# A gated recurrence in chunks: outputs of two heads as one block-diagonal product, and the next chunk's scores ahead of them

## The chip, the cores and the metric

The kernel runs on one core of a Trainium2 chip. The metric is the device time of one execution in microseconds (us); before the change it is the median of three runs. All matrix products are in fp32 on TensorE (PE in the profile). PSUM is the memory that PE writes, in eight banks; VectorE is DVE, ScalarE is ACT, GpSimd is POOL. In this program each engine has an instruction list of its own, carried out in order, and the lists meet at named semaphores.

## The reference

The program is a two-layer attention block followed by a block with three mixers and an MLP. The change lies in one mixer of the second block, the gated linear recurrence: 4 heads, 64 keys and 64 values each, 9 chunks of 128 tokens (the first holds padding and 16 meta tokens; its outputs are not used).

```python
def step(S, inp):
    q_c, k_c, v_c, g_c = inp
    gcum = jnp.cumsum(g_c, axis=1)
    seg = gcum[:, :, None] - gcum[:, None, :]
    decay = masked_decay(seg, causal[None, :, :, None, None])
    scores = jnp.einsum('bthk,btshk,bshk->btsh', q_c, decay, k_c)
    o_intra = jnp.einsum('btsh,bshv->bthv', scores, v_c)
    o_inter = jnp.einsum('bthk,bhkv->bthv', q_c * jnp.exp(gcum), S)
    k_end = k_c * jnp.exp(gcum[:, -1:] - gcum)
    S = S * jnp.exp(gcum[:, -1])[..., None] + jnp.einsum('bshk,bshv->bhkv', k_end, v_c)
    return S, o_intra + o_inter
```

## The kernel before

Everything here is in `stage_hg` (from L2653 on), where the list of each engine is written out by hand. The four heads are two pairs (`fb` 0 and 1); in a pair, head `e` has partitions 64*e to 64*e+63. The score of two tokens needs a decay that depends on both, so it is taken in levels: the chunk is halved again and again, and on each level queries and keys are scaled to the middle of their half. For chunk i the work is:

- `sums(i, fb)` (PE, L2670): three products of 384 columns into banks 0 to 2 give the sums of log decays on all levels. ACT takes their exponential (L2757, `EX`). DVE multiplies it with the queries (`q_levels`, L2799, `Qt`), POOL with the keys (L2785, `Kl`).
- `end_sums(i)` (PE, L2680): decays to the chunk's end, into columns 384 to 511 of banks 0 and 1; ACT's exponential (L2766, `EE`), then POOL's product with the keys (L2778, `kend`).
- `scores(i, fb)` (PE, L2693): 16 products, 8 for each head, with 64 rows each, into banks 4 to 7. There is one set of these banks, so the scores of a pair wait until DVE has taken the scores of the pair before.
- `merge(i, fb)` (DVE, L2816): 14 copies under a mask, 7 for each head, put the right level for every pair of tokens into `Sm`.
- `outputs(i, h)` (PE, L2711 and L2715), one head at a time: two products of `Sm` with the values (128 columns of moving data), and one of the scaled query with the head's state (64 rows, 64 columns), accumulated in bank 3. DVE copies the result out (L2836).
- the state sum (PE, L2745): `kend` times values, four products, into columns of banks 0 and 1; DVE scales the state and adds it (L2841, 64 columns for each pair).

A matrix product in the program is two MATMUL and two LDWEIGHTS instructions in the trace. `Sm` has one buffer, used by both pairs in turn, so `merge(i, 1)` waits for the first two outputs, which read pair 0's.

Of the kernel before, what the change touches and what calls it, by code (L numbers as in the profile page):

```python
# [15 lines left out]
ALU = mybir.AluOpType  # L16
# [4 lines left out]
P = 128  # L21
# [12 lines left out]
HD = 64  # L34
# [2618 lines left out]
def stage_hg(pr, qk, Kt, LF, Vh, OH, c, b_):  # L2653
# [8 lines left out]
    with nc.Block() as block:  # L2662
        @block.tensor
        def _(pe):
# [9 lines left out]
            def end_sums(i):  # L2674

                if i >= 1:
                    pe.wait_ge(*S["state_new"](i))
                    pe.wait_ge(*S["decayed"](2 * i + 2))
                for fb in range(2):
                    mm = pe.matmul(ps[:, fb, TW:BANK], c["gt"], LF[:, i, fb * P:(fb + 1) * P], start=True, stop=True)  # L2680
                mm.then_inc(*S["end_sums"].inc())
# [24 lines left out]
            def outputs(i, h):  # L2706
                fb, r = h // 2, slice(64 * (h % 2), 64 * (h % 2) + 64)
                j = (i - 1) * HGH + h
                pe.wait_ge(*S["masked"](4 * ((i - 1) * 2 + fb) + 3 + h % 2))
                for half in range(2):  # L2710
                    pe.matmul(ps[:, 3, h * P:h * P + WIDE], Sm[:, h % 2, half, :], Vh[:, i, h * HD:h * HD + WIDE],  # L2711
                              start=(half == 0), stop=False, skip_group_check=True)
                if j >= 1:
                    pe.wait_ge(*S["o_ready"](j))
                pe.matmul(ps[:, 3, h * P:h * P + HD], Qt[r, i % 2, fb, LEVELS, :], st[r, fb, :], start=False, stop=True,  # L2715
                          skip_group_check=True).then_inc(*S["o_ready"].inc())
# [3 lines left out]
            for i in range(n):  # L2720
                if i >= 1:
                    scores(i, 0)
                else:
                    pe.wait_ge(*S["decayed"](2))
                end_sums(i)
# [3 lines left out]
                if i >= 2:  # L2729
                    pe.wait_ge(*S["o_used"](i - 1))  # L2730
                if i >= 1:
                    outputs(i, 0)
                    scores(i, 1)
                if i + 1 < n:
                    sums(i + 1, 1)
                if i >= 1:
                    for h in range(1, HGH):
                        outputs(i, h)
                pe.wait_ge(*S["kend_ready"](i + 1))
                if i + 1 < n:  # L2740
                    pe.wait_ge(*S["decayed"](2 * i + 4))
                for fb in range(2):
                    for half in range(2):
                        at = fb * P + 64 * half
                        mm = pe.matmul(ps[64 * half:64 * half + 64, fb, TW:TW + HD], kend[:, at:at + 64], Vh[:, i, at:at + HD],  # L2745
                                       start=True, stop=True)
                mm.then_inc(*S["state_sum"].inc())
# [41 lines left out]
        def _(dve):  # L2789
            masks = c["pairs"].bitcast(mybir.dt.int32).rearrange("p (v n) -> p v n", v=LEVELS)  # L2790

            def q_levels(i, fb):
# [3 lines left out]
                if i >= 1:  # L2796
                    if i >= 3:
                        dve.wait_ge(*S["o_ready"](HGH * (i - 2)))
# [4 lines left out]
            def merge(i, fb):  # L2803
# [3 lines left out]
                for v in range(LEVELS):  # L2807
                    for e in range(2):
                        tile = (e, v % 2)
                        if v == 0:  # L2810
                            dve.wait_ge(*S["scored"](j + e + 1))
                            if j + e >= 2:
                                dve.wait_ge(*S["o_ready"](j + e - 1))
                        if tile in last:
                            dve.wait_ge(*S["dve"](last[tile]))
                        ins = dve.copy_predicated(Sm[:, e, v % 2, :], masks[:, v, :], ps[:, 4 + 2 * e + v // 4, v % 4 * P:(v % 4 + 1) * P])  # L2816
# [8 lines left out]
            dve.wait_ge(*S["state_zero"](2))  # L2825
            q_levels(0, 0)
            q_levels(0, 1)
            for i in range(n):
# [5 lines left out]
                if i >= 1:  # L2834
                    dve.wait_ge(*S["o_ready"](HGH * i))
                    dve.tensor_copy(OH[:, i - 1, :].rearrange("p (h d) -> p h d", h=HGH),  # L2836
# [362 lines left out]
```

## Time and profile before

| | us |
|---|---|
| median of three runs (lowest, highest) | 4134.05 (4129.21, 4137.35) |
| the profiled execution | 4127.2 |
| its span | 4125.4 |
| `stage_hg`, from its first matmul to its last state update | 171.48 |
| TensorE busy over the span | 3849.8 |
| TensorE busy in `stage_hg` | 139.29 |

The span runs from the first to the last recorded instruction of the profiled execution. A busy time sums instructions that may overlap between engines. The granted TensorE clock is a share of 2.4 GHz; its two levels are 1.0 and 0.5. DMA is idle in `stage_hg`: nothing is loaded there.

### The profile page before, as it was taken

The numbers are of one execution on the slowest core, as the hardware profiler recorded it, in microseconds if no ns is written. First come the engines' busy times: TensorE is split into PE (matmuls) and PEld (weight loads), VectorE is DVE, ScalarE is ACT, GpSimd is POOL, SyncE is SP. The second block draws the span as 40 slices with busy tenths as digits, with TensorE's granted clock in tenths as the row PEclk, the third lists the DMA queues.
The fourth block names the chain that finished last, engine by engine and source line by source line (L and its number), as shares of the span: only waits on it lengthen the run. The fifth ranks groups of instructions, "written<-read, shape, count | busy, mean of one in ns | idle before, by whom it ended". The sixth has DMA issues, their size and how long they took to land. (4 is left out here: it accounts for less than half of the span.)

```text
span 4125.4 us, 50459 instructions
## 1 busy us (share of the span) xinstructions
PE 3849.8 (93%) x19200; PEld 2376.3 (58%) x19200; DVE 2006.8 (49%) x4125; ACT 1284.2 (31%) x2388; POOL 698.3 (17%) x868
## 2 busy tenths in 40 slices
PE   5999999999998999899999899999787999999998
PEld 3655556756644655577565456656365488438843
DVE  3377456633534476465243303545244444674465
ACT  3245325523522344354243113442711211001100
POOL 2400230021004000501100001123032000430043
PEclk8999999999999999999999999999987999999999
DMA  4101240001021110100112200000100222452244
GB/s 176 44 19 37 103 149 16 2 16 68 25 71 41 52 37 27 66 1 1 36 48 72 72 31 21 21 21 1 41 1 22 89 90 97 163 183 98 86 163 153
DMA packets 108942, 253.71 MB, mean 61 GB/s; under 512 B 5200, under 2 KB 33872, under 8 KB 108320
## 3 DMA queue, kind: packets, MB, share of 16 engines
q1 hardware_dynamic: 103056, 231.86, 16.0%
q10 hardware_dynamic: 4384, 12.58, 0.8%
q0 software_dynamic: 1264, 6.04, 0.4%
q8 instruction: 156, 2.56, 0.3%
q14 instruction: 82, 0.67, 0.1%
HBM read 223.20 MB, written 27.26 MB: 61 GB/s over the span
## 5 line engine op out<-in xcount | busy, mean ns | idle before, releaser
L674 PE MATMUL ps<-ring,hT 128*128 128x384 f32 (+3 forms) x2208 | 692.4, 471 | 17.2 <-PEq L268 6.1
L674 PEld LDWEIGHTS ps<-ring,hT 128*128 128x128 f32 x2208 | 395.3, 195 | 274.0 <-issue 145.6
L1086 DVE TENSOR_REDUCE stat_a<-ps 128x1 f32<-128x1280 f32 (+1 forms) x144 | 196.6, 1368 | 178.9 <-PE ps L945 178.7
L984 PE MATMUL ps<-hT,ring 128*128 128x512 f32 (+1 forms) x640 | 280.2, 551 | 0.0
L1598 PE MATMUL ps<-ring,YT 128*128 128x512 f32 x576 | 250.2, 592 | 1.3 <-PEq L1363 1.3
L1026 ACT ACTIVATE YT<-ps,stat_a 128x1280 f32<-128x1280 f32 (+1 forms) x144 | 177.6, 1233 | 199.7 <-DVE stat_a L1086 197.7
L1962 ACT ACTIVATE hid<-hid 128x1024 f32<-128x1024 f32 x32 | 33.8, 1058 | 549.6 <-DVE hid L2042 549.6
L1982 POOL TENSOR_TENSOR Wd<-ring 128x512 f32<-128x512 f32 x64 | 85.5, 1335 | 678.1 <-DMA ring<-in_w_down 604.4
L1940 PE MATMUL ps<-Wd,const 128*128 128x512 f32 x384 | 185.9, 593 | 0.1
L1598 PEld LDWEIGHTS ps<-ring,YT 128*128 128x128 f32 x576 | 108.1, 190 | 131.4 <-issue 131.4
L1919 PE MATMUL ps<-Hc,Wu 128*128 128x256 f32 x768 | 171.0, 379 | 0.0
L441 PE MATMUL ps<-ring,hT 128*128 128x512 f32 (+1 forms) x432 | 160.1, 530 | 5.4 <-DMA ring<-in_w_in 5.1
L1919 PEld LDWEIGHTS ps<-Hc,Wu 128*128 128x128 f32 x768 | 145.9, 190 | 19.8
L1940 PE MATMUL ps<-ring,hid 128*128 128x512 f32 x256 | 133.3, 602 | 11.0 <-PE ps L1940 4.4
L1185 PE MATMUL ps<-qk_b 64*128 64x512 f32 (+1 forms) x600 | 124.0, 545 | 20.1 <-ACT P_b L1260 17.9
L1215 PE MATMUL ps<-const,P_b 128*128 128x128 f32 x984 | 136.6, 278 | 2.2 <-DVE YT L1125 1.8
L955 PEld LDWEIGHTS ps<-const,YT 128*128 128x128 f32 x656 | 69.1, 142 | 120.7 <-issue 105.1
L1250 ACT ACTIVATE PT_b<-ps 128x512 f32<-128x512 f32 x150 | 84.5, 596 | 166.0 <-PE ps L1215 166.0
L1919 PE MATMUL ps<-hT,ring 128*128 128x256 f32 x512 | 120.8, 390 | 15.7 <-DVE hT L2061 6.6
L1260 ACT ACTIVATE P_b<-ps,stat_b 128x1280 f32<-128x1280 f32 (+1 forms) x108 | 132.8, 1235 | 6.4 <-DVE stat_b L1300 6.4
L984 PEld LDWEIGHTS ps<-hT,ring 128*128 128x128 f32 x640 | 106.3, 191 | 40.1 <-issue 37.7
L2153 PE MATMUL ps<-hT,ring 128*128 128x348 f32 (+1 forms) x384 | 129.4, 466 | 0.0
(451 smaller groups left out, 6860.8 us busy)
## 6 DMA issues: line engine op xcount, KB each, us to landing
ring<-in_w_down SPq DMA_DIRECT2D x32, 2048.0 KB, 7.9
ring<-in_w_up SPq DMA_DIRECT2D x16, 2048.0 KB, 8.1
ring<-in_w_in SPq DMA_DIRECT2D x14, 2048.0 KB, 7.9
adaw_b<-in_w_ada SPq DMA_DIRECT2D x16, 1024.0 KB, 5.2
ring<-in_w_out SPq DMA_DIRECT2D x6, 2048.0 KB, 7.9
ring<-in_w_in SPq DMA_DIRECT2D x6, 1536.0 KB, 6.8
x<-res SPq DMA_DIRECT2D x18, 512.0 KB, 2.9
gates<-const SPq DMA_DIRECT2D x32, 256.0 KB, 2.4
```

What stands on the lines that cost most here:

```text
L441: mm = pe.matmul(ps[:, n % 2, 0:width], hT[:, k, t * P:(t + 1) * P], w[:, k, :], start=(k == 0), stop=(k == KC - 1))
L674: mm = pe.matmul(ps[:, n % 2, 0:hi - lo], hT[:, k, t * P:(t + 1) * P], w[:, k, lo:hi], start=(k == 0), stop=(k == KC - 1))
L984: mm = pe.matmul(ps[:, GB, 0:hi - lo], pr.view(i0 + c)[:, k, b % 4 * P:(b % 4 + 1) * P], hT[:, k, lo:hi], start=(k == 0), stop=(k == KC - 1))
L1026: act.activation(dst, scored_at(i, m), ACT.Exp, bias=st[:, i % 4, m:m + 1], accum_out=st[:, i % 4, 2 + m:3 + m])\
L1086: dve.tensor_reduce(st[:, i % 4, m:m + 1], scored_at(i, m), AX, ALU.max, negate=True)\
L1185: return pe.matmul(flat[:, at:at + width], qk[r, u["qb"], u["qt"] * P:(u["qt"] + 1) * P], qk[r, u["kb"], key:key + width], start=True, sto ...
L1215: mm = pe.transpose(ps[:, bank, (i - lo) * P:(i - lo + 1) * P], Pb[:, p % 2, e, b * P:(b + 1) * P], ident)
L1260: act.activation(Pb[:, p % 2, e, 0:nk[p] * P], scored_at(p, e), ACT.Exp, bias=st[:, p % 4, e:e + 1], accum_out=st[:, p % 4, 2 + e:3 + e]). ...
L1598: mm = pe.matmul(ps[:, 2 * (m % 2) + h, :], YT[:, k, t * P:(t + 1) * P], w[:, k, :], start=(k == 0), stop=(k == KC - 1))
L1919: mm = pe.matmul(up_at(n, x), a[:, k, :], b[:, k, :], start=(k == 0), stop=(k == 3))
L1940: mm = pe.matmul(ps[:, down_bank(pair, x), :], a, b, start=(j == 0), stop=(j == PAIRS - 1))
L2153: mm = pe.matmul(ps[:, dense_bank(u), 0:hi - lo], w[:, k, (b % 4) * P:(b % 4 + 1) * P], hT[:, k, lo:hi], start=(k == 0), stop=(k == KC - 1))
```

## The change

Both pairs get their own half of `Sm` (`[P, 2, 2, 2, P]`). The state becomes a tile of 128 columns for each pair, with the two heads' blocks on its diagonal and zeros elsewhere. `outputs(i, fb)` does a pair at a time: one product with 128 rows and 128 columns takes both heads' scaled queries through the state, and four products of 64 columns add `Sm` times values. The state sums move from banks 0 and 1 into the free half of bank 3, whose off-diagonal blocks are cleared once; the state update now reads 128 columns for each pair. TensorE's list is written in another order: the first scores of chunk i + 1 and its end sums come ahead of the second outputs and the state sum of chunk i. DVE's copy of the outputs comes behind its wait for the state sum.

```diff
@@ -2673,9 +2673,7 @@
...
-                if i >= 1:
-                    pe.wait_ge(*S["state_new"](i))
-                    pe.wait_ge(*S["decayed"](2 * i + 2))
+                pe.wait_ge(*S["decayed"](2 * i + 2))
                 for fb in range(2):
@@ -2703,48 +2701,49 @@
...
-            def outputs(i, h):
-                fb, r = h // 2, slice(64 * (h % 2), 64 * (h % 2) + 64)
-                j = (i - 1) * HGH + h
-                pe.wait_ge(*S["masked"](4 * ((i - 1) * 2 + fb) + 3 + h % 2))
-                for half in range(2):
-                    pe.matmul(ps[:, 3, h * P:h * P + WIDE], Sm[:, h % 2, half, :], Vh[:, i, h * HD:h * HD + WIDE],
-                              start=(half == 0), stop=False, skip_group_check=True)
-                if j >= 1:
-                    pe.wait_ge(*S["o_ready"](j))
-                pe.matmul(ps[:, 3, h * P:h * P + HD], Qt[r, i % 2, fb, LEVELS, :], st[r, fb, :], start=False, stop=True,
-                          skip_group_check=True).then_inc(*S["o_ready"].inc())
+            def outputs(i, fb):
+                if fb == 0:
+                    pe.wait_ge(*S["state_new"](i))
+                pe.wait_ge(*S["masked"](4 * place(i - 1, fb)))
+                pe.matmul(ps[:, 3, fb * P:(fb + 1) * P], Qt[:, i % 2, fb, LEVELS, :], st[:, fb, :], start=True, stop=False,
+                          skip_group_check=True)
+                for h in range(2 * fb, 2 * fb + 2):
+                    for half in range(2):
+                        mm = pe.matmul(ps[:, 3, h * HD:(h + 1) * HD], Sm[:, fb, h % 2, half, :], Vh[:, i, h * HD:(h + 1) * HD],
+                                       start=False, stop=(half == 1), skip_group_check=True)
+                mm.then_inc(*S["o_ready"].inc())
+            def state_sum(i):
+                pe.wait_ge(*S["kend_ready"](i + 1))
+                for fb in range(2):
+                    for half in range(2):
+                        r, at = slice(64 * half, 64 * half + 64), fb * P + 64 * half
+                        mm = pe.matmul(ps[r, 3, 2 * P + at:2 * P + at + HD], kend[:, at:at + 64], Vh[:, i, at:at + HD],
+                                       start=True, stop=True, skip_group_check=True)
+                mm.then_inc(*S["state_sum"].inc())
...
             sums(0, 1)
-            for i in range(n):
-                if i >= 1:
-                    scores(i, 0)
-                else:
-                    pe.wait_ge(*S["decayed"](2))
-                end_sums(i)
+            end_sums(0)
+            pe.wait_ge(*S["end_decayed"](1))
+            sums(1, 0)
+            sums(1, 1)
+            scores(1, 0)
+            end_sums(1)
+            pe.wait_ge(*S["state_zero"](3))
+            state_sum(0)
+            for i in range(1, n):
                 if i + 1 < n:
...
                     sums(i + 1, 0)
-                if i >= 2:
-                    pe.wait_ge(*S["o_used"](i - 1))
-                if i >= 1:
-                    outputs(i, 0)
-                    scores(i, 1)
+                scores(i, 1)
+                outputs(i, 0)
                 if i + 1 < n:
                     sums(i + 1, 1)
-                if i >= 1:
-                    for h in range(1, HGH):
-                        outputs(i, h)
-                pe.wait_ge(*S["kend_ready"](i + 1))
-                if i + 1 < n:
-                    pe.wait_ge(*S["decayed"](2 * i + 4))
-                for fb in range(2):
-                    for half in range(2):
-                        at = fb * P + 64 * half
-                        mm = pe.matmul(ps[64 * half:64 * half + 64, fb, TW:TW + HD], kend[:, at:at + 64], Vh[:, i, at:at + HD],
-                                       start=True, stop=True)
-                mm.then_inc(*S["state_sum"].inc())
+                    scores(i + 1, 0)
+                    end_sums(i + 1)
+                outputs(i, 1)
+                state_sum(i)
@@ -2787,6 +2786,7 @@
...
         def _(dve):
+            sums_at = ps[:, 3, 2 * P:BANK]
             masks = c["pairs"].bitcast(mybir.dt.int32).rearrange("p (v n) -> p v n", v=LEVELS)
@@ -2795,7 +2795,7 @@
...
                     if i >= 3:
-                        dve.wait_ge(*S["o_ready"](HGH * (i - 2)))
+                        dve.wait_ge(*S["o_ready"](place(i - 3, fb)))
                     dve.tensor_tensor(Qt[:, i % 2, fb, :, :], EX[:, fb, 0:LEVELS + 1, :],
@@ -2809,11 +2809,11 @@
...
                             dve.wait_ge(*S["scored"](j + e + 1))
-                            if j + e >= 2:
-                                dve.wait_ge(*S["o_ready"](j + e - 1))
+                            if i >= 2:
+                                dve.wait_ge(*S["o_ready"](place(i - 2, fb)))
                         if tile in last:
                             dve.wait_ge(*S["dve"](last[tile]))
-                        ins = dve.copy_predicated(Sm[:, e, v % 2, :], masks[:, v, :], ps[:, 4 + 2 * e + v // 4, v % 4 * P:(v % 4 + 1) * P])
+                        ins = dve.copy_predicated(Sm[:, fb, e, v % 2, :], masks[:, v, :], ps[:, 4 + 2 * e + v // 4, v % 4 * P:(v % 4 + 1) * P])
                         if v < LEVELS - 2:
@@ -2822,7 +2822,8 @@
...
             dve.memset(st[:], 0.0).then_inc(*S["state_zero"].inc())
-            dve.wait_ge(*S["state_zero"](2))
+            dve.memset(sums_at, 0.0).then_inc(*S["state_zero"].inc())
+            dve.wait_ge(*S["state_zero"](3))
             q_levels(0, 0)
@@ -2831,15 +2832,14 @@
...
                         q_levels(i + 1, fb)
-                if i >= 1:
-                    dve.wait_ge(*S["o_ready"](HGH * i))
-                    dve.tensor_copy(OH[:, i - 1, :].rearrange("p (h d) -> p h d", h=HGH),
-                                    ps[:, 3, :].rearrange("p (h d) -> p h d", h=HGH)[:, :, 0:HD]).then_inc(*S["o_used"].inc())
                 dve.wait_ge(*S["q_levels"](place(i, 1)))
                 dve.wait_ge(*S["state_sum"](i + 1))
+                if i >= 1:
+                    dve.wait_ge(*S["o_ready"](place(i - 1, 1)))
+                    dve.tensor_copy(OH[:, i - 1, :], ps[:, 3, 0:2 * P])
                 for fb in range(2):
                     ins = dve.scalar_tensor_tensor(out=st[:, fb, :], in0=st[:, fb, :], scalar=dec[:, i % 2, fb:fb + 1],
-                                                   in1=ps[:, fb, TW:TW + HD], op0=ALU.mult, op1=ALU.add)
+                                                   in1=sums_at[:, fb * P:(fb + 1) * P], op0=ALU.mult, op1=ALU.add)
                 ins.then_inc(*S["state_new"].inc())
@@ -3132,7 +3132,7 @@
...
                         "decay": sv("decay", P, 2, 2), "EE": sv("EE", P, 256), "kend": sv("kend", P, 256),
-                        "Sm": sv("Sm", P, 2, 2, P), "state": sv("state", P, 2, HD)})
+                        "Sm": sv("Sm", P, 2, 2, 2, P), "state": sv("state", P, 2, P)})
             with ExitStack() as w:
...
```

TensorE in the middle of the stage, before: from the second sums of a chunk (L2670) over the outputs of three heads (L2711, L2715) and the state sum (L2745) to the first scores of the next (L2693).

```order
L2670 MATMUL ps<-const,LF_hg 128x384 x3
L2711 MATMUL ps<-V,Sm_hgc 128x128 x2
L2715 MATMUL ps<-state_hgc,hT 128x64
L2711 MATMUL ps<-V,Sm_hgc 128x128 x2
L2715 MATMUL ps<-state_hgc,hT 128x64
L2711 MATMUL ps<-V,Sm_hgc 128x128 x2
L2715 MATMUL ps<-state_hgc,hT 128x64
L2745 MATMUL ps<-V,kend_hgc 64x64 x4
L2693 MATMUL ps<-hT 128x128 x2
L2693 MATMUL ps<-hT 64x64 x2
L2693 MATMUL ps<-hT 128x128 x10
L2693 MATMUL ps<-qk_hg 128x128 x2
```

The same stretch after the change; L2691 are scores, L2678 end sums, L2708 and L2712 the two kinds of output product, L2721 the state sum.

```order
L2670 MATMUL ps<-const,LF_hg 128x384 x3
L2691 MATMUL ps<-hT 128x128 x2
L2691 MATMUL ps<-hT 64x64 x2
L2691 MATMUL ps<-hT 128x128 x10
L2691 MATMUL ps<-qk_hg 128x128 x2
L2678 MATMUL ps<-LF_hg,const 128x128 x2
L2708 MATMUL ps<-state_hgc,hT 128x128
L2712 MATMUL ps<-V,Sm_hgc 128x64 x4
L2721 MATMUL ps<-V,kend_hgc 64x64 x4
L2670 MATMUL ps<-const,LF_hg 128x384 x3
```

The first scores and the end sums of the next chunk stand between the second sums and the outputs of the second pair; these outputs are one product and four instead of three times two and one.

DVE in the same stretch with what it waits for, before: the masks of the second pair, the query levels, the copy of the outputs (L2836), the state update (L2841), the next masks.

```order
L2816 COPY_PREDICATED Sm_hgc<-const,ps 128x128 [waits o_ready,scored] x2
L2816 COPY_PREDICATED Sm_hgc<-const,ps 128x128 x2
L2816 COPY_PREDICATED Sm_hgc<-const,ps 128x128 [waits dve] x10
L2799 TENSOR_TENSOR hT<-EX_hgc,qk_hg 128x1024 [waits o_ready,decayed]
L2801 COPY decay_hgc<-EX_hgc 128x1
L2836 COPY O_hg<-ps 128x256 [waits o_ready]
L2841 SCALAR_TENSOR_TENSOR state_hgc<-state_hgc,decay_hgc,ps 128x64 [waits state_sum,q_levels]
L2841 SCALAR_TENSOR_TENSOR state_hgc<-state_hgc,decay_hgc,ps 128x64
L2816 COPY_PREDICATED Sm_hgc<-const,ps 128x128 [waits o_ready,scored,state_new]
```

After the change:

```order
L2816 COPY_PREDICATED Sm_hgc<-const,ps 128x128 [waits o_ready,scored] x2
L2816 COPY_PREDICATED Sm_hgc<-const,ps 128x128 x2
L2816 COPY_PREDICATED Sm_hgc<-const,ps 128x128 [waits dve] x10
L2799 TENSOR_TENSOR hT<-EX_hgc,qk_hg 128x1024 [waits o_ready,decayed]
L2801 COPY decay_hgc<-EX_hgc 128x1
L2839 COPY O_hg<-ps 128x256 [waits o_ready,state_sum,q_levels]
L2841 SCALAR_TENSOR_TENSOR state_hgc<-state_hgc,decay_hgc,ps 128x128 x2
L2816 COPY_PREDICATED Sm_hgc<-const,ps 128x128 [waits o_ready,scored,state_new]
```

The order is the same; the copy of the outputs now also waits for the state sum, and the update has 128 columns.

## Rows read from the trace of the kernel before

**Rows 1.** The page's busy times over the span.

```profile
PE 3849.8 (93%) x19200; PEld 2376.3 (58%) x19200; DVE 2006.8 (49%) x4125; ACT 1284.2 (31%) x2388; POOL 698.3 (17%) x868
```

**Rows 2.** Stretches of the stage: PE, PEld, DVE, ACT, POOL busy, clock, DMA, GB/s.

```profile
2979.65:3151.13 171.48, 139.29 (x920) 104.45 (x920) 75.14 (x286) 23.82 (x27) 48.86 (x25) 0.82 0.00 1
3021.04:3033.71 12.67, 10.04 (x69) 7.36 (x69) 6.92 (x26) 2.26 (x2) 5.87 (x3) 1.00 0.01 2
3110.60:3131.10 20.50, 17.39 (x115) 13.43 (x113) 9.22 (x35) 2.65 (x3) 5.88 (x3) 0.75 0.00 1
3131.10:3151.13 20.03, 15.05 (x102) 12.56 (x100) 7.21 (x33) 0.38 (x1) 0.73 (x1) 0.67 0.00 1
```

**Rows 3.** Waits in the stage: who for whom, total us, times, longest.

```profile
PE ps L2711 <- DVE Sm_hgc L2816: 22.8, 9, 2.6
DVE Sm_hgc L2816 <- PE ps L2715: 20.2, 8, 2.7
```

**Rows 4.** Timeline of one chunk at full clock: start, us, instruction, [idle before].

```profile
3021.04 2.21 PE L2670 MATMUL ps<-const,LF_hg 128*128 128x384 f32 x6 [0.47 <-ACT EE_hgc L2766]
3023.08 0.61 PE L2711 MATMUL ps<-V,Sm_hgc 128*128 128x128 f32 x4
3023.28 1.13 ACT L2757 ACTIVATE EX_hgc<-ps 128x1152 f32<-128x1152 f32 x1 [2.29 <-PE ps L2670]
3023.63 0.37 PE L2693 MATMUL ps<-hT 64*128 64x128 f32 x1
3024.44 1.22 DVE L2799 TENSOR_TENSOR hT<-EX_hgc,qk_hg 128x1024 f32<-128x1024 f32 x1 [1.93 <-ACT EX_hgc L2757]
3026.05 2.21 PE L2670 MATMUL ps<-const,LF_hg 128*128 128x384 f32 x6
3026.16 0.30 DVE L2816 COPY_PREDICATED Sm_hgc<-const,ps 128x128 f32<-128x128 int32 x1 [0.42 <-PE ps L2693]
3029.17 2.67 DVE L2816 COPY_PREDICATED Sm_hgc<-const,ps 128x128 f32<-128x128 int32 x13 [2.71 <-PE ps L2715]
3031.70 0.71 PE L2711 MATMUL ps<-V,Sm_hgc 128*128 128x128 f32 x4 [2.63 <-DVE Sm_hgc L2816]
3033.71 0.54 PE L2745 MATMUL ps<-V,kend_hgc 128*64 128x64 f32 x8
3033.82 0.42 DVE L2836 COPY O_hg<-ps 128x256 f32<-128x256 f32 x1 [0.79 <-PE ps L2715]
3034.17 3.48 PE L2693 MATMUL ps<-hT 64*128 64x128 f32 x28
3034.35 0.47 DVE L2841 SCALAR_TENSOR_TENSOR state_hgc<-state_hgc,decay_hgc,ps 128x64 f32<-128x64 f32 x2
3037.80 0.71 PE L2680 MATMUL ps<-LF_hg,const 128*128 128x128 f32 x4
3038.99 0.59 PE L2670 MATMUL ps<-const,LF_hg 128*128 128x384 f32 x1 [0.47 <-ACT EE_hgc L2766]
```

**Rows 5.** Timeline, the same operations in stretches of half clock.

```profile
2989.18 3.87 PE L2670 MATMUL ps<-const,LF_hg 128*128 128x384 f32 x6 [0.47 <-ACT EE_hgc L2766]
3015.49 3.64 PE L2693 MATMUL ps<-hT 64*128 64x128 f32 x28
3019.48 0.79 PE L2680 MATMUL ps<-LF_hg,const 128*128 128x128 f32 x2
3128.71 0.93 PEld L2711 LDWEIGHTS ps<-V,Sm_hgc 128*128 128x128 f32 x4
```

**Rows 6.** Timeline of earlier stages: products of narrow and of 128-column data.

```profile
517.49 0.61 PE L631 MATMUL ps<-const,row_b 128*128 128x2 f32 x4
517.95 1.10 PE L674 MATMUL ps<-ring,hT 128*128 128x512 f32 x2
...
2810.48 1.89 PE L2557 MATMUL ps<-xdt_ssd,W_ssd 128*128 128x128 f32 x16
```

**Rows 7.** Timeline, the first product of key levels on POOL.

```profile
2994.30 3.11 POOL L2785 TENSOR_TENSOR hT<-EX_hgc,qk_hg 128x896 f32<-128x896 f32 x1 [4.36 <-ACT EX_hgc L2757]
```

## The prediction

> **What bounds the kernel now.** I began with the page's busy times: TensorE is busy in 3849.8 of 4125.4 us [rows 1], so it sets the time of the program as a whole, and only what it does or waits for inside the changed stage counts. The stretches of the stage come next. It takes 171.48 us, 4.2% of the span. TensorE's records cover 139.29 us of it, DVE's 75.14, and the granted clock is 0.82, which with levels of 1.0 and 0.5 (2.4 and 1.2 GHz) means half clock in 36% of the time [rows 2]. DMA moves nothing there. Then the waits: DVE's masks wait 20.2 us for the outputs of the pair before, which still read `Sm`, and TensorE's outputs then wait 22.8 us for the masks [rows 3]. That is one stall of about 2.6 us a chunk.
>
> The timeline of a chunk shows what ends last. In the stretch from 3021.04 to 3033.71 the granted clock is 1.00 [rows 2]. TensorE runs without a break from the level sums to the output of the second head; DVE's masks start at 3029.17, and TensorE's outputs go on at 3031.70 after 2.63 us of nothing [rows 4]. One more wait of 0.47 us stands in each chunk between the end sums and the next level sums, for ACT's exponential [rows 4]. At 3034.17 comes the next chunk.
>
> The length of a chunk at full clock, from these rows: 3034.17 - 3021.04 = 13.13 us; the scores, 3026.05 - 3023.63 = 2.42; end sums and the wait for ACT, 3038.99 - 3037.80 = 1.19. Together 16.74 us [rows 4]. The measured length is (3131.10 - 3015.49) / 6 = 19.27 us [rows 2, 5]. So half clock costs 2.53 us a chunk.
>
> **The change, part by part.** Durations at full clock.
>
> *Outputs.* Before, two heads take 3033.71 - 3031.70 = 2.01 us, and the first head of a chunk 0.55 (3023.08 to 3023.63), since scores start beside its last product: 0.55 + 3 x 1.0 = 3.55 us a chunk [rows 4]. Now a pair is 5 products, 10 instructions. Four of the five move 64 columns instead of 128. Does this halve them? Products with 128 columns of weights and only 2 moving columns stand 0.46 / 4 = 0.115 us apart, and those with 128 moving columns take at most 1.89 / 16 = 0.118 [rows 6]. The loading of weights sets the pace, so the narrow ones gain nothing. I take 0.112 each, 1.12 a pair, and 0.17 for the change between 64 and 128 rows: a head has six instructions, 0.67, in its 1.0, and the other 0.33 lies in two such changes. So 1.29 a pair, 2.58 a chunk: 0.97 less on TensorE. Bounds for a pair: 0.7 (the eight narrow ones at half the pace, 2 x 0.112 + 8 x 0.056) and 2.01 (what two heads take now).
>
> By the Trainium skill, "TensorE: Matmul & The Clock Gate", section "Back-to-back issue gap", a matmul of up to 64 columns takes about 60 cycles, under half of one with 128; its section "LDWEIGHTS (loading the stationary operand)" has the load go by weight columns, 128 here whatever moves. By the first a pair would take 0.4 us less and the total some 5 us less; the trace agrees with the second, with 0.115 us for 2 moving columns [rows 6].
>
> *The order.* Call T the start of `scores(i, 0)`. Then, on TensorE: scores 2.42, end sums 4 x 0.112 = 0.45, outputs of pair 1 of the chunk before 1.29, and 0.64 from the start of the state sum to when DVE can read it (3033.71 to 3034.35) [rows 4]: T + 4.80. DVE, whose list has the copy and the state update ahead of the next masks, stands idle until then, though the scores were ready at T + 2.53 (3023.63 to 3026.16). Its copy takes 0.45, the update of twice 128 columns 0.60 (bounds 0.47, what two of 64 take now, and 0.84, two copies of 256 columns) and 0.10 to settle: masks start at T + 5.95. They take 2.87 (2.67 for 13 and 0.20 for one) [rows 4], to T + 8.82. TensorE meanwhile does the state sum and the next level sums, 2.04 (3021.04 to 3023.08) [rows 4], to T + 6.7, and must wait for the masks, since `scores(i, 1)` go into the same banks: idle for 2.15 us. Scores from T + 8.85, masks of pair 1 from 11.38 to 14.25. TensorE: 8.85 + 2.42 + 1.29 + 2.04 = 14.60. The later of the two, 14.60, is the next T. So both chains are nearly even, and the stall has not gone: it was 2.63 + 0.47 and is 2.15, and it now stands before `scores(i, 1)`.
>
> The gain of structure is 16.74 - 14.60 = 2.1 us a chunk: 0.97 of outputs, 0.95 of waits, the rest of changes of shape. What would be late next is covered: the level sums that end at T + 6.7 give an exponential (1.13) by T + 8.1 [rows 4], and POOL's product, 3.11 at most [rows 7], ends by T + 11.3, ahead of 14.60. DVE's own (1.22) lies between the two sets of masks, 8.82 to 11.38 [rows 4]. ACT's exponential of the end sums is done before T + 4, so that the level sums no longer wait for it.
>
> *End sums in bank 0 and 1, state sums in bank 3.* The end sums lose their wait for the state update, which was never last. No cost either way: DVE reads bank 3 (T + 4.8 to 5.9) while TensorE writes bank 0.
>
> *More to clear.* 512 more columns of `Sm` and 256 of bank 3. A DVE operation on 256 columns takes 0.42 [rows 4], so under 1.3 us, while TensorE does the first level sums, up to 3.87 at half clock [rows 5]. Nothing.
>
> *Start.* The first product of levels on POOL ends at 2994.30 + 3.11 = 2997.41 [rows 7]; `scores(1, 0)` start at 2997.45. The state sum comes behind scores and end sums, at 3000.4, DVE's update ends at 3001.7, masks 3004.5, scores, then 2.42 + 1.29 + 2.04 for TensorE: `scores(2, 0)` at 3010.3. Before: 3015.49 [rows 5]. 5.2 us earlier.
>
> *End.* From the eighth chunk's T: masks of pair 1 end at 14.25, outputs 1.29, state sum 0.64, copy and update 1.05: 17.2. Before it was 20.03 at a clock of 0.67 [rows 2]. With some half clock I take 18.8: 1.2 less.
>
> *The clock.* This is the unknown. Half clock costs 2.53 us a chunk now, with 3.1 us idle. In proportion to the idle time it would cost 2.53 x 2.15 / 3.1 = 1.8. Below, 0: the clock stays up. Above, 4. I take 1.8, the value nearest to the rows, since the stall is nearly as long as the one after which the clock falls today. A chunk is then 16.4 us, six chunks 98.4 against 115.6.
>
> *Sum.* 5.2 + 17.2 + 1.2 = 23.6 us less. The stage would take 148 us. The profiled execution took 4127.2 us and would take 4103.6. It lies 6.85 below the median of the three runs; 4134.05 - 23.6 gives 4110.
>
> **The rivals.**
>
> *A: the clock stays up.* Before the stall the scores take 2.42 in all, at 3034.17, behind it, 3.48 for all but the last four instructions [rows 4]: the clock falls after the stall. If 2.15 us are too short for a fall, a chunk takes 14.6: six are 87.6, 28.0 less; start 5.2, end 2.8. 36 us less, 4098. For it: shorter idle time in one piece. Against it: it is only 0.5 us shorter than the longest one now. In the Trainium skill, "TensorE: Matmul & The Clock Gate", section "Loop structure matters more than you think", the clock stays up when matmuls follow each other densely; by that rule moving scores into the gap would give this case. That the trace has a clock of 1.00 up to the stall and 3.48 us for scores behind it [rows 2, 4] agrees, but the new order keeps a stall.
>
> *B: more half clock than now.* Each chunk has work that DVE's chain waits for right behind the stall (`scores(i, 1)`), so a fall there lengthens both chains. At 3 to 4 us of loss a chunk takes 17.6 to 18.6: 4 to 10 less over six; with start and end 8 to 16 us less, 4122. For it: at half clock level sums take 3.87 and scores 3.64 and more [rows 5]. Against: the idle time of a chunk is 1 us less than now.
>
> *C: slower.* The stage falls to half clock for good. Then scores take 3019.48 - 3015.49 = 3.99, level sums 3.87, four output instructions 0.93, so ten and a shape change 2.6 [rows 5]. To T': 3.99 + 0.9 + 2.6 + 0.8 = 8.3, copy, update and masks 4.0, scores 3.99, outputs 2.6, level sums 3.87: 22.8 us a chunk, 3.5 more than the 19.27 now. Six: 21 more, and at the ends what order gains, half clock takes: 4155. It decides when half clock fills over 57% of a chunk ((19.27 - 14.6) / (22.8 - 14.6)). The last chunks now stand at 0.75 and 0.67 [rows 2], 50% and 66% of half clock, which keeps this alive; but these are after longer stalls.
>
> *D: only TensorE's work counts.* If DVE's update or its masks start later than I think, by more than 1.5 us, the whole gain of order is lost and the 0.97 x 8 = 8 us of outputs are left: 4126.
>
> **How the numbers follow.** The forecast has a chance of 0.60 (15 to 31 us less, 4103 to 4119), A 0.16, B 0.11, D 0.08, C 0.05. The range is 4096 to 4124: it holds the forecast, most of A and part of B, and about 0.15 is left out. This kernel's runs spread by 0.2% (8 us), which I take for what can be told from no change. Faster by over that: forecast, A and most of B, 0.86. Within it: D and a rest of B, 0.09. Slower: C, 0.05.
>
> **What would show it.** In the changed profile: ten output instructions in about 1.1 us, not 0.7; the outputs' wait for masks gone, and a wait of about 2.1 us of the scores of pair 1 in its place; DVE idle for over 3 us in each chunk until the state sum; chunks of 14.6 us where the clock is 1.00; a granted clock over the stage near 0.85. Wrong would be a chunk of over 16 us at full clock, a wait of the scores for POOL's levels, or a clock below 0.7.

## The result, and the profile after

| | before | after |
|---|---|---|
| median, us (lowest, highest; runs) | 4135.7 (4129.21, 4137.45; 4) | 4103.7 (4099.38, 4111.16; 4) |
| ratio to before (95% interval) | 1 | 0.9927 (0.9909, 0.9946) |
| profiled execution, us (span) | 4127.2 (4125.4) | 4111.16 (4109.3) |
| `stage_hg`, us | 171.48 | 144.38 |
| behind the stage to the span's end, us | 974.3 | 973.8 |

The forecast, 4110 in 4096 to 4124, came from the first three runs before; the table has a fourth. Run again beside the experiments the changed kernel gave 0.9936 (0.9920, 0.9952) and a stage of 144.35.

The two profiled spans differ by 16 us, the stages by 27: the stage begins at 2991.15 in this profile and at 2979.65 in that of before, so the part ahead of it, which the change does not touch, took 11.5 us more. In the repetition the stage began at 2989.23, and in the kernels below between 2979 and 2994. This is the spread of the program's first 3 ms, and it is why the stage is compared below, beside the times.

Stretches of the changed kernel (columns as in [rows 2]): the stage, a chunk at full clock, a chunk with half clock in it, the end.

```profile
2991.15:3135.53 144.38, 119.09 (x888) 86.64 (x888) 84.34 (x287) 23.82 (x27) 50.22 (x25) 0.87 0.00 1
3071.93:3085.90 13.97, 12.01 (x110) 9.06 (x109) 10.60 (x35) 2.65 (x3) 5.92 (x3) 1.00 0.00 1
3024.83:3042.06 17.23, 15.27 (x110) 11.21 (x109) 10.69 (x35) 2.65 (x3) 5.92 (x3) 0.80 0.00 1
3117.09:3135.53 18.44, 12.06 (x115) 10.61 (x114) 8.91 (x36) 1.51 (x2) 3.84 (x2) 0.77 0.00 1
```

The granted clock is 0.87 against 0.82, so half clock has fallen from 62 us to 144.38 x 0.13 x 2 = 38 us. TensorE is busy 119.09 us instead of 139.29. What waits now, in the stage:

```profile
PE ps L2691 <- DVE Sm_hgc L2816: 17.7, 8, 4.1
DVE O_hg L2839 <- PE ps L2721: 15.9, 8, 2.3
```

The outputs' 22.8 us for the masks [rows 3] are gone, but for 1.25 us in the last chunk. In their place stand 17.7 us in which the scores wait for masks, and 15.9 us in which DVE's copy of the outputs waits for the state sum. The chunk at full clock, the counterpart of [rows 4]:

```profile
3071.93 2.07 PE L2691 MATMUL ps<-hT 64*128 64x128 f32 x28
...
3074.15 0.71 PE L2678 MATMUL ps<-LF_hg,const 128*128 128x128 f32 x4
3074.30 0.15 DVE L2801 COPY decay_hgc<-EX_hgc 128x1 f32<-128x1 f32 x1
...
3074.70 0.39 PE L2708 MATMUL ps<-state_hgc,hT 128*128 128x128 f32 x2
...
3074.92 1.00 PE L2712 MATMUL ps<-V,Sm_hgc 128*128 128x64 f32 x8
...
3075.85 0.45 PE L2721 MATMUL ps<-V,kend_hgc 128*64 128x64 f32 x8
...
3076.23 2.21 PE L2670 MATMUL ps<-const,LF_hg 128*128 128x384 f32 x6
...
3076.41 0.42 DVE L2839 COPY O_hg<-ps 128x256 f32<-128x256 f32 x1 [1.95 <-PE ps L2721]
3076.75 0.60 DVE L2841 SCALAR_TENSOR_TENSOR state_hgc<-state_hgc,decay_hgc,ps 128x128 f32<-128x128 f32 x2
3077.38 2.87 DVE L2816 COPY_PREDICATED Sm_hgc<-const,ps 128x128 f32<-128x128 int32 x14
...
3080.40 2.07 PE L2691 MATMUL ps<-hT 64*128 64x128 f32 x28 [1.96 <-DVE Sm_hgc L2816]
...
3082.62 0.49 PE L2708 MATMUL ps<-state_hgc,hT 128*128 128x128 f32 x2
...
3083.79 2.16 PE L2670 MATMUL ps<-const,LF_hg 128*128 128x384 f32 x6
...
3085.90 0.38 PE L2691 MATMUL ps<-hT 64*128 64x128 f32 x2
```

Scores of the next chunk at 3071.93, DVE free at 3074.45 (3074.30 + 0.15), and then nothing on DVE until the state sum at 3075.85 lets the copy go at 3076.41. The masks of those scores start only at 3077.38; TensorE has meanwhile done the level sums and stands idle for 1.96 us until 3080.40, when the last mask has freed the score banks. The next chunk begins at 3085.90: 13.97 us.

### The profile page after: what moved, and what is told of

Its sections match the earlier page's. It is cut to its first block and busy times, and to the rows that moved or that the text cites. A ratio compares the mean times of both kernels' runs of the same rounds, so it can differ in the third digit from the quotient of the medians.

```text
span 4109.3 us, 50380 instructions
## 1 busy us (share of the span) xinstructions
PE 3842.2 (93%) x19168; PEld 2364.6 (58%) x19168; DVE 2019.3 (49%) x4126; ACT 1284.0 (31%) x2388; POOL 697.0 (17%) x868
## 5 line engine op out<-in xcount | busy, mean ns | idle before, releaser
L674 PE MATMUL ps<-ring,hT 128*128 128x384 f32 (+3 forms) x2208 | 694.3, 472 | 17.2 <-PEq L268 6.1
L1940 PE MATMUL ps<-ring,hid 128*128 128x512 f32 x256 | 133.6, 603 | 11.2 <-PE ps L1940 4.4
```

The source lines that it names most:

```text
L674: mm = pe.matmul(ps[:, n % 2, 0:hi - lo], hT[:, k, t * P:(t + 1) * P], w[:, k, lo:hi], start=(k == 0), stop=(k == KC - 1))
L1940: mm = pe.matmul(ps[:, down_bank(pair, x), :], a, b, start=(j == 0), stop=(j == PAIRS - 1))
```

## The experiments

All stage times are from one profile each, from the first matmul of `stage_hg` to its last state update. The kernels ran in three sets, each with the kernel before beside them, and the ratio is against that one: 4130.40 us for the change, old order, masks first and the stall filled with eight, 4132.44 for own masks, heads apart, the wide outputs and the old stall filled, 4128.13 for the other two fills. So kernels of different sets are compared by their ratios.

| kernel | TensorE's order | outputs | stage, us | clock | chunk at full clock | median, us | ratio (95%) |
|---|---|---|---|---|---|---|---|
| before | old | head by head | 171.48 | 0.82 | 16.46 (the prediction has 16.74) | see above | 1 |
| own masks | old | head by head | 130.70 | 0.96 | 13.75 | 4088.89 | 0.9895 (0.9880, 0.9910) |
| old order | old, but for one output | pair at once | 129.93 | 0.95 | 13.51 | 4090.45 | 0.9905 (0.9890, 0.9921) |
| heads apart | new | head by head | 153.84 | 0.88 | none | 4116.81 | 0.9961 (0.9946, 0.9976) |
| the change | new | pair at once | 144.38 | 0.87 | 13.97 | 4107.28 | 0.9936 (0.9920, 0.9952) |
| masks first | new | pair at once | 116.18 | 0.97 | 11.98 | 4076.51 | 0.9864 (0.9850, 0.9879) |

The 16.46 is measured with the old stall filled (e6_before_fill, below); no chunk of the kernel before is at full clock from end to end. In the row of the change the stage is the first profile's, the median and ratio are the repetition's.

Three stretches of the stage are used below: the start, up to `scores(2, 0)`; the middle, the six chunks from there to `scores(8, 0)`; and the end.

**Repetition of the change (r1_after).**

> The changed kernel again, as the measure for the runs beside it. By the theory that the stage alone moved (171.48 to 144.4 us in the two profiles): 27 us less than before, ratio 0.9935. By a rival that something else than the stage moved as well: a ratio of 0.9925 or lower here too, with a stage of 144 us.

0.9936 and 144.35 us, so 27 us, as the first theory has it. The first comparison's 0.9927 lies within its interval.

**The old order with the new tiles (e2_old_order).**

```diff
-            scores(1, 0)
-            end_sums(1)
             pe.wait_ge(*S["state_zero"](3))
             state_sum(0)
             for i in range(1, n):
+                scores(i, 0)
+                end_sums(i)
                 if i + 1 < n:
                     pe.wait_ge(*S["end_decayed"](i + 1))
                     sums(i + 1, 0)
-                scores(i, 1)
                 outputs(i, 0)
+                scores(i, 1)
                 if i + 1 < n:
                     sums(i + 1, 1)
-                    scores(i + 1, 0)
-                    end_sums(i + 1)
                 outputs(i, 1)
                 state_sum(i)
```

> The new tiles (own masks' buffer for each pair, block-diagonal state, outputs of two heads at once, state sums in bank 3), but TensorE's list in the old order. Theory: the order gives nothing of itself; the masks of pair 1 can start as soon as its scores are there, so the old stall shrinks from 2.6 to about 1 us, and a chunk at full clock takes 2.04 (level sums) + 1.26 (outputs) + 2.3 (scores) + 2.04 + about 1.0 of stall + 1.26 + 0.38 + 2.3 + 1.19 (end sums and ACT) = 13.8 us, as much as the 13.97 of the changed kernel; time within 5 us of the changed kernel. Rival: the order is what brings the gain, then a chunk is 15.5 us or more at full clock and the time 12 us or more above the changed kernel.

13.51 us a chunk, but not the same time: 14.4 us less than the changed kernel in the stage, and 16.8 us less in the median of the same set. The theory was right that the order gives nothing, and too kind to it: it costs. Of the 14.4 us, 11.2 lie in the six middle chunks, 92.26 us in the change against 81.06: at full clock the new order costs 0.46 us a chunk, 2.8 us in six, and the other 8.4 are the clock, 0.91 there against 1.00. Start and end give 2.2 and 1.0. The list differs from the old one in one place: the outputs of the second head stand ahead of `scores(i, 1)`, since a pair is now done at once. The idle time of this kernel comes in two small pieces, 0.47 and 0.82 us:

```profile
3041.02 2.21 PE L2670 MATMUL ps<-const,LF_hg 128*128 128x384 f32 x6 [0.47 <-ACT EE_hgc L2763]
...
3046.45 2.21 PE L2670 MATMUL ps<-const,LF_hg 128*128 128x384 f32 x6
3046.55 2.87 DVE L2814 COPY_PREDICATED Sm_hgc<-const,ps 128x128 f32<-128x128 int32 x14 [0.84 <-PE ps L2691]
...
3049.48 0.49 PE L2708 MATMUL ps<-state_hgc,hT 128*128 128x128 f32 x2 [0.82 <-DVE Sm_hgc L2814]
```

**Only the masks' buffer (e7_own_masks).** The kernel before, with this:

```diff
-        "Sm": sv("Sm", P, 2, 2, P)
+        "Sm": sv("Sm", P, 2, 2, 2, P)
-        pe.matmul(..., Sm[:, h % 2, half, :], ...)
+        pe.matmul(..., Sm[:, fb, h % 2, half, :], ...)
-        if j + e >= 2:
-            dve.wait_ge(*S["o_ready"](j + e - 1))
+        if i >= 2:
+            dve.wait_ge(*S["o_ready"](j + e + 1 - HGH))
-        dve.copy_predicated(Sm[:, e, v % 2, :], ...)
+        dve.copy_predicated(Sm[:, fb, e, v % 2, :], ...)
```

> The kernel before with one edit: each pair of heads has its own buffer for the merged scores, so the masks of pair 1 no longer wait for outputs of pair 0. Outputs, state and orders as before. Theory: this buffer alone takes away the stall of 2.63 us (masks of pair 1 start 3.0 us earlier and end where the outputs of the second head end), a chunk takes 16.74 - 2.6 = 14.1 us at full clock and the clock stays up: stage 135 to 141 us, as fast as the whole change (144.4) or faster. Rival: the stall comes back elsewhere (scores of the next chunk, DVE), a chunk at full clock stays over 15.5 us and the stage over 155.

130.70 us, below the range, and faster than the whole change (0.9895 against 0.9936, with intervals that do not meet). One timeline, columns as in [rows 4]:

```profile
3050.74 2.21 PE L2670 MATMUL ps<-const,LF_hg 128*128 128x384 f32 x6
3050.84 2.88 DVE L2816 COPY_PREDICATED Sm_hgc<-const,ps 128x128 f32<-128x128 int32 x14 [0.42 <-PE ps L2693]
...
3052.78 0.61 PE L2711 MATMUL ps<-V,Sm_hgc 128*128 128x128 f32 x4
...
3053.32 0.43 PE L2715 MATMUL ps<-state_hgc,hT 64*128 64x64 f32 x2
...
3053.68 0.71 PE L2711 MATMUL ps<-V,Sm_hgc 128*128 128x128 f32 x4
```

All 14 masks of pair 1 start at 3050.84, right behind their scores, and TensorE goes from the output of the second head (3053.32) to that of the third (3053.68) without a wait. Before it was 2.63 us [rows 4].

**Heads apart in the new order (e1_heads_apart).**

```diff
-        pe.matmul(ps[:, 3, fb * P:(fb + 1) * P], Qt[:, i % 2, fb, LEVELS, :], st[:, fb, :], ...)
         for h in range(2 * fb, 2 * fb + 2):
             ...
+            if j >= 1:
+                pe.wait_ge(*S["o_ready"](j))
+            pe.matmul(ps[:, 3, h * HD:(h + 1) * HD], Qt[r, i % 2, fb, LEVELS, :], st[r, fb, at:at + HD], ...)
```

> The changed kernel with the outputs of each head by itself again (two products of masked scores and one of 64 rows with the head's state, with the semaphore between heads), everything else as changed. Theory: a pair takes 2.0 us instead of 1.26, both pairs are on TensorE's path, so a chunk takes 13.97 + 1.5 = 15.5 us at full clock; stage 154 to 160 us instead of 144.4. Rival: the outputs are covered by DVE's masks, at most 0.8 us a chunk more, stage 151 at most.

153.84 us, 9.5 more than the change and just below the range. The outputs of a pair take 1.79 and 1.90 us (3018.41 to 3020.20, 3028.51 to 3030.41) instead of 1.15 and 1.17, so 1.37 more for both: on TensorE's path, as the theory has it. There is no chunk at full clock here; the clock falls behind the stall in each of the six middle chunks, which take 16.97 us in the mean against 15.38.

In the old order the same outputs gain little, since there the masks of pair 1 end last: a chunk has 13.51 us instead of 13.75 (old order against own masks), and most of what they save turns into the wait of 0.82. Whether that makes the kernel faster is not shown: the stages are 0.8 us apart, from one profile each, and the ratios stand the other way, 0.9905 against 0.9895, with overlapping intervals. The two kernels also differ in the place of the state sums and of DVE's copy, which no run separates.

**The narrow outputs widened (e3_wide).** The columns of the neighbouring head get other sums here.

```diff
-    mm = pe.matmul(ps[:, 3, h * HD:(h + 1) * HD], Sm[:, fb, h % 2, half, :], Vh[:, i, h * HD:(h + 1) * HD], ...)
+    at = min(h, 2) * HD
+    mm = pe.matmul(ps[:, 3, at:at + WIDE], Sm[:, fb, h % 2, half, :], Vh[:, i, at:at + WIDE], ...)
```

> The changed kernel with 128 instead of 64 moving columns in the four products of masked scores with values (the neighbour head's columns get wrong sums). Theory: the load of 128 weight columns sets the pace, so ten output instructions still take 1.12 us at full clock and the time is the same within 3 us. Rival: the narrow ones are faster by up to half; then a pair takes 0.4 us more here, a chunk 0.8, and the stage 6 us more.

At full clock the theory holds: eight wide ones take 3093.69 - 3092.70 = 0.99 us, eight narrow ones in the changed kernel 3075.85 - 3074.92 = 0.93, and the load of weights sets the pace.

```profile
3092.70 1.06 PE L2713 MATMUL ps<-V,Sm_hgc 128*128 128x128 f32 x8
3093.69 0.45 PE L2722 MATMUL ps<-V,kend_hgc 128*64 128x64 f32 x8
...
3098.24 2.07 PE L2691 MATMUL ps<-hT 64*128 64x128 f32 x28 [1.96 <-DVE Sm_hgc L2817]
```

The stage is not the same within 3 us: 135.29 us, 9 less than the change, with twice the columns moved in these products, a stall of 1.96 us as before and a clock of 0.93 instead of 0.87 (row below). That the wide products did this is not shown. The profiles part before the first of them: the third level sums take 2.21 us here (from 2996.81) and 3.90 in the change (from 3000.57), with the same instructions ahead. And the ratio, 0.9917 (0.9903, 0.9932) at 4097.83 us, has an interval that overlaps that of the change.

**The stall filled (e4_fill, e8_fill_half), and the same work put elsewhere (e9_fill_elsewhere).** Here `fill` is a row of products of 128 columns whose results are overwritten. The three kernels in one diff, with comments that are not in the kernels:

```diff
+                pe.wait_ge(*S["state_new"](i))
+                fill(i, 8, 0)        # e8: 4 of them
                 scores(i, 1)
                 outputs(i, 0)
+                fill(i, 8, P)        # e9: here alone, without the wait
```

> The changed kernel with 8 more products of 128 columns (about 1.8 us at full clock, results not used) in the stall before the scores of pair 1, behind a wait for the state update, which is ready by then. Theory: the stall of 1.96 us is what lowers the clock; filled, the granted clock of the middle chunks is 1.0, chunks take 14.0 us throughout, and the stage 137 to 141 us instead of 144. Rival: the clock falls for what the matmuls themselves are (narrow outputs, 64-row scores); then the fall stays and the fill lengthens each half-clock chunk by up to 2 us, the stage takes 146 or more.

> The changed kernel with 4 instead of 8 extra products in the stall before the scores of pair 1 (0.9 us at full clock, so 1.06 us of the stall stays). Theory: a stall of about 1 us in one piece, as in the kernel with the new tiles in the old order (0.82), does not lower the clock; chunks of 14.0 us, half clock in under 15 us of the stage, stage 131 to 135 us. Rival: the clock needs the whole stall filled; then half clock stays above 25 us and the stage at 138 or more.

> The changed kernel with the same 8 extra products, but after the outputs of pair 0 and not in the stall: the stall of 1.96 us stays, and TensorE's path gets 1.8 us longer in each chunk. Theory: it is the stall that lowers the clock; half clock stays at 25 us or more of the stage and chunks take 15.8 us and more, stage 155 us or more. Rival: what counts is the work in a chunk as a whole; then half clock shrinks to under 12 us as with the filled stall, and the stage takes 143 to 148 us.

**The old stall filled (e6_before_fill).** The kernel before, with `fill(i, 10, 2 * P)` ahead of `outputs(i, 2)`.

> The kernel before with 10 more products of 128 columns (2.24 us at full clock, results not used) in the stall before the outputs of the third head. Theory: half clock costs the kernel before 2.5 us a chunk and comes from this stall; filled, the middle chunks take 16.7 to 16.9 us and the stage 150 to 156 us instead of 171.5, though TensorE does more work. Rival: the clock falls anyway, then the stage stays at 168 or more.

The stages of these, in the order e4, e8, e9, e6, e3, a fence for each kernel:

```profile
2983.72:3115.72 132.00, 120.53 (x1016) 92.83 (x1016) 84.12 (x287) 23.82 (x27) 50.24 (x25) 0.97 0.00 1
```
```profile
2983.60:3117.79 134.19, 116.91 (x952) 88.91 (x952) 84.11 (x287) 23.80 (x27) 50.23 (x25) 0.93 0.00 1
```
```profile
2994.28:3145.93 151.65, 127.62 (x1016) 98.40 (x1016) 84.44 (x287) 23.82 (x27) 50.21 (x25) 0.91 0.00 1
```
```profile
2988.98:3141.95 152.97, 139.87 (x1080) 107.69 (x1080) 75.20 (x286) 23.79 (x27) 48.92 (x25) 0.95 0.00 1
```
```profile
2986.80:3122.09 135.29, 110.25 (x888) 81.40 (x888) 84.23 (x287) 23.80 (x27) 50.24 (x25) 0.93 0.00 1
```

Eight extra products in the stall make the stage 12.4 us shorter (132.00; median 4093.13, 0.9906 (0.9891, 0.9921)), at a chunk of 13.97 as before: below the range expected, and all of it the clock, 0.97. Four do nearly as well (134.19; 4093.54, 0.9911 (0.9896, 0.9926)), with a stall of 1.07 us left, once 1.44. Half clock is 134.19 x 0.07 x 2 = 19 us there, not under 15 as expected; but the six middle chunks are at 1.00, as with eight, and it lies in the start and the end. The same eight outside the stall cost: 151.65 us (4116.77, 0.9963 (0.9949, 0.9977)), less than the 155 expected. Half clock is 151.65 x 0.09 x 2 = 27 us, above the 25 of the theory, and a chunk at full clock 15.73. In the kernel before the fill takes 18.5 us off the stage (152.97; 4119.92, 0.9966 (0.9954, 0.9977)). Its chunk of 16.46 us, with the masks and outputs at the same distances as before, is the chunk of the kernel before at full clock: half clock cost that one 19.27 - 16.46 = 2.8 us a chunk.

So the long stall is what brings half clock into the middle of the stage. In the six kernels where no stall of the middle chunks is over 1.44 us (own masks, old order, masks first, the two fills of the new stall, the old stall filled) these chunks are at 1.00. In the five with a stall of 1.96 us or more in each chunk the clock falls in some or all of the six: in all six of the kernel before (2.63 us) and of heads apart (1.96), in three of the change, four with the fill elsewhere, one with the wide outputs (all 1.96, once 2.3). Scores and level sums show it, 2.07 and 2.16 us at full clock; here for the change, then four fills, then heads apart:

```profile
3033.30 2.33 PE L2691 MATMUL ps<-hT 64*128 64x128 f32 x28 [1.96 <-DVE Sm_hgc L2816]
...
3038.18 3.95 PE L2670 MATMUL ps<-const,LF_hg 128*128 128x384 f32 x6
...
3094.37 2.07 PE L2691 MATMUL ps<-hT 64*128 64x128 f32 x28 [1.96 <-DVE Sm_hgc L2816]
...
3097.76 2.16 PE L2670 MATMUL ps<-const,LF_hg 128*128 128x384 f32 x6
```
```profile
3022.54 2.07 PE L2691 MATMUL ps<-hT 64*128 64x128 f32 x28 [1.07 <-DVE Sm_hgc L2822]
```
```profile
3024.75 3.44 PE L2691 MATMUL ps<-hT 64*128 64x128 f32 x28 [1.96 <-DVE Sm_hgc L2818]
```

Which of these stalls brings a fall is open. More work beside the stall does not settle it: the extra products elsewhere go with a clock of 0.91 over the stage, the longer outputs of heads apart with 0.88, the change with 0.87.

**DVE's list mended (e5_masks_first).** The masks of pair 0 come ahead of the copy and the state update of the chunk before. The lines taken out (`...`: the waits for the query levels, the state sum and the outputs, the copy, the update) are now the body of `update(i)`.

```diff
             for i in range(n):
                 for fb in range(2):
                     if i >= 1:
                         merge(i, fb)
+                        if fb == 0:
+                            update(i - 1)
                     if i + 1 < n:
                         q_levels(i + 1, fb)
-                ...
+            update(n - 1)
```

> The changed kernel with DVE's list in another order: the masks of pair 0 ahead of the copy of the outputs and the state update of the chunk before. Theory: the stall before the scores of pair 1 comes from DVE standing idle for the state sum (1.9 to 2.3 us each chunk) while the scores of pair 0 are ready; without that a chunk takes 12.0 us at full clock (13.97 - 1.96), TensorE has no stall and the clock stays up: stage 122 to 128 us, 17 to 22 us below the changed kernel. Rival: TensorE's own list or POOL's key levels bound the chunk, then it stays at 13.5 us or more and the time within 5 us of the changed kernel.

The stage takes 116.18 us, 28 below the change, more than expected by 6: the six middle chunks give 20.4 us, the start 2.9 and the end 5.0. This is the fastest version, 4076.51 us.

```profile
3049.88 2.07 PE L2691 MATMUL ps<-hT 64*128 64x128 f32 x28
...
3052.11 0.71 PE L2678 MATMUL ps<-LF_hg,const 128*128 128x128 f32 x4
...
3052.30 2.86 DVE L2816 COPY_PREDICATED Sm_hgc<-const,ps 128x128 f32<-128x128 int32 x14
...
3053.81 0.45 PE L2721 MATMUL ps<-V,kend_hgc 128*64 128x64 f32 x8
...
3054.19 2.21 PE L2670 MATMUL ps<-const,LF_hg 128*128 128x384 f32 x6
...
3055.06 0.41 DVE L2828 COPY O_hg<-ps 128x256 f32<-128x256 f32 x1
3055.40 0.59 DVE L2830 SCALAR_TENSOR_TENSOR state_hgc<-state_hgc,decay_hgc,ps 128x128 f32<-128x128 f32 x2
...
3056.33 0.75 PE L2691 MATMUL ps<-hT 64*128 64x128 f32 x8
```

The masks start at 3052.30, 0.19 us behind the first end sum that follows their scores (3052.11), the copy and the update stand behind them at 3055.06, and TensorE goes from the level sums into `scores(i, 1)` at 3056.33 without a wait. A chunk is 3061.87 - 3049.88 = 11.99 us, 11.98 in the mean of six, and TensorE is busy for all of it. The same edit to DVE's list with TensorE's list in the old order was not run, so it is not shown whether the new order is worth having once DVE's list fits it.

## Why the prediction was right, and where it was not

*The mechanism of the path* held: the stall moved to `scores(i, 1)`, it is 1.96 us against 2.15, and DVE stands idle until the state sum. A chunk at full clock was put at 14.60 and takes 13.97. The terms were mostly a little long: scores 2.22 (3071.93 to 3074.15) instead of 2.42, since the 2.42 of [rows 4] had a state product of the old outputs in its beginning; outputs of a pair 1.15 and 1.17 (3074.70 to 3075.85, 3082.62 to 3083.79) against 1.29; from the copy's start to the masks' 0.97 against 1.15, with the update of 128 columns 0.60 as taken and 0.03 behind it where 0.10 "to settle" was put in without a row.

Two readings of DVE's list were wrong without harm. Its idle time before the copy was to be over 3 us and is 1.95, since the second product of query levels (3073.16, 1.23 us) falls into it, which the working did not have. And the one between the two sets of masks was priced at 1.22 us and takes 2.75 (3080.16), for it starts behind POOL's product (last section); the masks of pair 1 start at 3082.89, 0.27 us behind the end of their scores at 3082.62.

*The chunk before* was put at 16.74 at full clock and is 16.46, by the filled old stall. The 0.28 too much are the 0.20 in the scores and 0.08 in the state sum, which takes 0.46 from 3033.71 to 3034.17 in [rows 4] and 0.38 at full clock. So half clock cost the kernel before 2.81 us a chunk and not 2.53, and the change gains 2.49 in structure, where 2.14 was forecast.

*The clock* was taken at 1.8 us a chunk in the changed kernel. The mean chunk is (3117.09 - 3024.83) / 6 = 15.38, so it was 1.41. Rival A, that it stays up, was wrong: 0.80 in the chunk from 3024.83. Three chunks in a row are at full clock, though, behind the same stall as the others. The 1.8 was a proportion to the idle time, without a mechanism; that the mean came within 0.4 us of it is partly luck, since single chunks lost between 0 and 3.3 us. Rival B, a chunk of 17.6 to 18.6, is excluded by the mean of 15.38. Rival C (half clock for good) and D (DVE later than thought) did not come.

*Start* was put at 5.2 us and gave 2.2 (3024.83 - 2991.15 = 33.68 against 35.84). The step up to `scores(1, 1)` was right, 7.1 us after `scores(1, 0)` (3008.96 to 3016.07, forecast 7.05). The 3.0 us lost lie behind it, where 8.76 us to `scores(2, 0)` stand against a forecast of 5.8 (3004.5 to 3010.3): the forecast had full clock there, and the outputs take 2.18 us and the level sums 4.05 to the next scores.

```profile
3020.78 4.11 PE L2670 MATMUL ps<-const,LF_hg 128*128 128x384 f32 x6
```

*End*: 1.6 against 1.2. The sum is 2.2 + 6 x 3.89 + 1.6 = 27.1 against 23.6. The six chunks were the term that was too small, 17.2 where the profiles have 23.3, and the start was too large, so the sum is nearer than its terms: that part is luck. The median moved by 32 and, as ratios have it, by 26 to 30.

*What the prediction missed* is which edit earns. It gave 0.97 us a chunk to outputs and 0.95 to less waiting, and said of the order that the stall had not gone. The runs say more: the buffer of its own for each pair's masks, in the prediction only a line of the description, takes 40.8 us off the stage by itself (171.48 to 130.70). With the outputs of a pair at once and the new places of state sums and copy it stands at 129.93, no clear difference, and the new order puts 14.4 back (144.38), which leaves the 27.1. So the size of the gain was forecast, and its source was not: the two parts that the prediction priced, outputs and order, give nothing clear and a loss when each is taken by itself behind the buffer. By the timelines the order costs since it puts the scores of the next chunk ahead of the state sum on TensorE, while DVE's list still has its wait for that sum ahead of the masks of these scores; with DVE's list mended the stage falls to 116.18.

## What to carry to other kernels

Try a change's parts one by one: here one buffer gave more than the whole. When an engine's list is reordered so that a result comes early, look at the list of the engine that takes it, and at what that list waits for first. Here a stall of 1.96 us on TensorE cost its length and, by a lower clock, 1.41 us more in the mean chunk; with the stall filled by useless products the stage was 12 us shorter. But fill a stall only when it can't be removed: removing it gave 28.

## What the hardware showed that was not expected

- Useless products can pay: 12.4 us off the stage in the changed kernel and 18.5 in the one before. They have to stand in the stall: the same eight elsewhere made the stage 7.3 us longer.
- The same stall of 1.96 us brings half clock in one chunk and none in the next: of the six middle chunks, in three in the change, in six with heads apart. Stalls of 1.07 us, once 1.44, brought none (clock 1.00).
- Moving 128 columns instead of 64 with the same weights cost 0.06 us for eight instructions at full clock.
- Where a product of DVE and one of POOL overlap, the one that starts second takes longer. In the changed kernel POOL's key levels start at 3079.75 and take 2.08, and DVE's query levels, begun at 3080.16, take 2.75. At 3073.16 DVE is first: 1.23, and POOL's, begun at 3073.21, take 3.12.

```profile
3073.16 1.23 DVE L2799 TENSOR_TENSOR hT<-EX_hgc,qk_hg 128x1024 f32<-128x1024 f32 x1 [1.38 <-ACT EX_hgc L2756]
3073.21 3.12 POOL L2784 TENSOR_TENSOR hT<-EX_hgc,qk_hg 128x896 f32<-128x896 f32 x1 [5.36 <-ACT EX_hgc L2756]
...
3079.75 2.08 POOL L2784 TENSOR_TENSOR hT<-EX_hgc,qk_hg 128x896 f32<-128x896 f32 x1 [2.63 <-ACT EX_hgc L2756]
3080.16 2.75 DVE L2799 TENSOR_TENSOR hT<-EX_hgc,qk_hg 128x1024 f32<-128x1024 f32 x1
```
